# The fourth column group of the down and output products: one 512-column and one 256-column matmul per row block instead of three of 256

## The reference

```python
h = h + g2_l * swiglu_ffn(ada_norm(h, norm_ffn[i], sh2_l, sc2_l), ffn_w_in[i], ffn_w_out[i])   # dn1
h = h + jnp.einsum('bse,ed->bsd', mix, w_out_even[i])                                           # oe
h = h + gated_conv_ffn(hn, w_ffn_gate[layer], ..., w_ffn_down[layer])                           # dn2, dn3
h = h + jnp.einsum('bse,ed->bsd', mix, w_out_odd[i])                                            # oo
```

## Time and profile before

| | us |
|---|---|
| median of three runs | 1526.22 |
| profiled execution, its own time | 1526.18 |
| its span, first to last instruction | 1524.6 |
| PE busy | 1510.4 |
| PE weight loads busy | 1260.0 |
| DVE busy | 938.5 |
| ACT busy | 711.2 |

### The profile page before, as it was taken

One profiled execution on the slowest core, in us unless ns is written; L12 is line 12 of the kernel. 1 busy time (PEld: TensorE's weight loads), 2 busy tenths in 40 slices (PEclk: granted clock), 3 DMA queues, 4 the chain that ended last, 5 costly groups with the idle time before them and its releaser, 6 DMA issues.

```text
span 1524.6 us, 21609 instructions
## 1 busy us (share of the span) xinstructions
PE 1510.4 (99%) x9039; PEld 1260.0 (83%) x9039; DVE 938.5 (62%) x1234; ACT 711.2 (47%) x1002; POOL 76.2 (5%) x103
## 2 busy tenths in 40 slices
PE   7999999999999999999999999999999999999998
PEld 5777657778888888879778888899888899988887
DVE  6332585553424342466877667669789855779973
ACT  5411585342213222245764455545656546556553
POOL 0220041000000000000010000033000000000000
PEclk9999999999999999999999999999999999999999
DMA  9776424452532232453145555665555564565552
GB/s 359 239 206 222 121 32 168 164 194 85 191 111 83 85 108 90 158 194 111 56 166 177 184 188 171 220 201 194 175 197 181 194 193 150 182 203 170 195 191 83
DMA packets 244256, 251.38 MB, mean 165 GB/s; under 512 B 17229, under 2 KB 237744, under 8 KB 244160
## 3 DMA queue, kind: packets, MB, share of 16 engines
q1 hardware_dynamic: 242624, 247.48, 49.3%
q0 software_dynamic: 928, 1.87, 0.4%
q10 hardware_dynamic: 608, 0.66, 0.1%
HBM read 248.94 MB, written 1.05 MB: 164 GB/s over the span
## 4 chain that ended last, share of the span: by engine, by line
PE 98%; DMA 1%; DVE 0%; ACT 0%; issue 0%; SPq 0%; DVEq 0%; ACTq 0%
PE psum L394 95%; PE psum L995 3%; DMA vtok<-in_ctx 1%; PE psum L966 0%; PE psum L563 0%; ACT scr L674 0%; PE psum L2471 0%; DVE sums L1106 0%; ACT L680 0%; PE psum L2351 0%; DVE y L2517 0%; DVE scr L754 0%; DVE xl L745 0%; DVE pt L1128 0%; SPq L298 0%
## 5 line engine op out<-in xcount | busy, mean ns | idle before, releaser
L380 DVE TENSOR_TENSOR wl<-raw,wh 128x2048 fp32r<-128x2048 f32 (+1 forms) x183 | 413.6, 2262 | 251.6 <-ACT wh L373 251.4
L373 ACT ACTIVATE wh<-raw 128x2048 fp32r<-128x2048 f32 (+1 forms) x183 | 344.3, 1883 | 332.8 <-PE psum L394 285.3
L394 PE MATMUL psum<-x,wh 128*128 128x512 f32 (+1 forms) x1520 | 461.6, 364 | 0.0
L394 PE MATMUL psum<-x,wl 128*128 128x256 f32 x1312 | 367.5, 280 | 0.0
L394 PEld LDWEIGHTS psum<-x,wh 128*128 128x128 f32 x1520 | 271.7, 189 | 48.5 <-issue 1.4
L394 PEld LDWEIGHTS psum<-x,wl 128*128 128x128 f32 x1312 | 248.3, 189 | 0.0
L394 PE MATMUL psum<-xh,wh 128*128 128x512 f32 (+1 forms) x624 | 240.5, 385 | 0.3 <-DVE xl L745 0.3
L394 PE MATMUL psum<-xl,wh 128*128 128x512 f32 (+1 forms) x624 | 236.9, 380 | 0.0
L394 PE MATMUL psum<-xh,wl 128*128 128x512 f32 (+1 forms) x624 | 236.8, 380 | 0.0
L394 PEld LDWEIGHTS psum<-xh,wh 128*128 128x128 f32 x624 | 118.1, 189 | 29.4 <-DVE xl L586 4.3
L394 PEld LDWEIGHTS psum<-xh,wl 128*128 128x128 f32 x624 | 118.0, 189 | 22.0
(11 more groups left out here) (290 smaller groups left out, 1990.4 us busy)
## 6 DMA issues: line engine op xcount, KB each, us to landing
raw<-in_ffn_w_in SPq DMA_DIRECT2D x44, 1024.0 KB, 5.0
pre<-in_ada_w SPq DMA_DIRECT2D x27, 1024.0 KB, 9.7
raw<-in_w_ffn_gate SPq DMA_DIRECT2D x22, 1024.0 KB, 5.0
raw<-in_w_ffn_up SPq DMA_DIRECT2D x22, 1024.0 KB, 5.0
raw<-in_ada_w SPq DMA_DIRECT2D x21, 1024.0 KB, 5.4
raw<-in_w_ffn_down SPq DMA_DIRECT2D x19, 1024.0 KB, 4.7
raw<-in_ffn_w_out SPq DMA_DIRECT2D x16, 1024.0 KB, 4.6
raw<-in_na_w_qkv SPq DMA_DIRECT2D x10, 1024.0 KB, 6.6
```

The costliest lines, as they stand in the source:

```text
L373: act.e.activation(wh[:, c % NSPL, 0:z], raw[:, p % NRAW, 0:z], ACT.Copy).then_inc(W.hi, 1)
L380: dve.e.tensor_tensor(wl[:, c % NSPL, 0:z], raw[:, p % NRAW, 0:z], wh[:, c % NSPL, 0:z].bitcast(F32), ALU.subtract).then_inc(W.lo, 1)
L394: return pe.e.matmul(o, l, r, start=start, stop=stop, skip_group_check=shared)
```

## The change

`Down` gets a parameter `wides`, the number of column groups that run wide: four unless said otherwise, three for `o1`, none without a wide operand. `down_pe` and `down_dve` ask for `i < d.wides` where they asked for `i < 3`, and the count of `half` is that of `wides`. So the fourth group of `dn1`, `oe`, `dn2` and `oo` goes through `group_wide` into two banks (6 and 7, 6 and 7, 4 and 5, 6 and 7), and its result is added to the residual in two parts. Everything else stays.

```diff
-            def __init__(self, name, pieces, banks, src, free, gates, gain, to, n, double=False, wide=None):
+            def __init__(self, name, pieces, banks, src, free, gates, gain, to, n, double=False, wide=None, wides=4):
...
-                self.per = 2 if gates else 1
+                self.per, self.wides = 2 if gates else 1, wides if wide is not None else 0
...
-                mine = (3 * self.per if wide is not None else 0, 4 * self.per, ...)
+                mine = (self.wides * self.per, 4 * self.per, ...)
...
         def down_pe(d, ready, ks=None):
             for i in range(4):
                 d.free(i)
-                if d.wide is not None and i < 3:
+                if i < d.wides:
                     group_wide([psum[:, d.banks[i] + m, :] for m in range(2)], d.chunks(i), d.wide, ready, k_outer=i == 0, ks=ks)
...
                 b = bank[d.banks[i]]
-                if d.wide is not None and i < 3:
+                if i < d.wides:
                     parts = [psum[:, d.banks[i]:d.banks[i] + 2, s * T:s * T + T] for s in range(2)]
...
-        O1 = Down("o1", 1, (0, 2, 4, 0), (xh4, xl4), free_o1, (1, 2), None, None, 3, wide=x4)
+        O1 = Down("o1", 1, (0, 2, 4, 0), (xh4, xl4), free_o1, (1, 2), None, None, 3, wide=x4, wides=3)
```

More of the change, by code:

```diff
@@ L1692, in program @@
         class Down:
-            def __init__(self, name, pieces, banks, src, free, gates, gain, to, n, double=False, wide=None):
+            def __init__(self, name, pieces, banks, src, free, gates, gain, to, n, double=False, wide=None, wides=4):
                 self.name, self.pieces, self.banks, self.src, self.free, self.gates, self.wide = name, pieces, banks, src, free, gates, wide
                 self.gain, self.to, self.n, self.double = gain, to, n, double
-                self.per = 2 if gates else 1
+                self.per, self.wides = 2 if gates else 1, wides if wide is not None else 0
                 self.at = downs[-1]
-                mine = (3 * self.per if wide is not None else 0, 4 * self.per, 8 if to else 0, 8 if to and to[1] is not None else 0, 12 if double else 4, 4, 4 if double else 0)
+                mine = (self.wides * self.per, 4 * self.per, 8 if to else 0, 8 if to and to[1] is not None else 0, 12 if double else 4, 4, 4 if double else 0)
                 downs.append(DN._make(a + b for a, b in zip(self.at, mine)))
```

## The result

The changed kernel takes 1529.48 us (median of 13 runs, 1528.41 to 1531.05) against 1526.74 us for the kernel before (13 runs, 1524.23 to 1527.10). The ratio is 1.0025, with a 95% interval of 1.0018 to 1.0032: slower by about 3.8 us (the two medians stand 2.7 us apart), where 1.4 us less was forecast. The profiled execution took 1530.46 us, with a span of 1528.9 us, 4.3 us more than before.

What follows compares the result with a forecast made beforehand. The prediction took PE's stream of matmul pitches as the bound. A gain of 1.47 us less 0.05 us of waiting made -1.42 us, from 1526.22 us to 1524.8 us; the range was 1523.7 to 1526.4 us.

Steps and rivals of the forecast that it cites:

- The gain of the fourth groups: Fourth groups of `dn1`, `oe`, `dn2`, `oo` would take as long as their wide third groups: 1.47 us less.
- The border behind `dn1`: From `dn1` to `even`, PE's spare time before lo of block 6 shrinks to 0.03 us; 0.05 us waiting, bounds 0 and 0.3.
- The other three borders: Behind `oe`, `dn2` and `oo`, the added DVE work of 0.73 us each stays covered, so PE doesn't wait.
- the last of `dn1`'s sums: DVE's sums before PE's statistics behind `dn1`: 2.09 us spare before the change, 1.02 after.
- the span is the sum of PE's matmul pitches, and an edit is worth what it takes out of PE's stream, unless it makes PE wait: Whole kernel: PE's chain is 98% PE, so the edit's worth is PE time removed, 1.47 us, less any new waiting.
- a little slower for a reason that the trace doesn't show: Wide pairs in `oe` took 0.3525 us against 0.3466 in `dn1`; used for the gain's lower end, 0.9 us.
- Columns alone count: PE's column count is unchanged, so no gain: 1526.2 us; chance 0.10 together with the case of covers eaten.
- The chain behind the last add: PE waits for second half-add, hi and lo at all four borders: 3.1 us cost, 1527.8 us; chance 0.04.
- A load paid in full: Each of 120 removed PE weight loads saves its own 189 ns, 22.7 us in all: 1503.5 us; chance 0.01.

Runs made afterwards that it cites:

- SPREAD = 2: The changed kernel with the two transposes that spread the norm factor in `up2` and `up3` two wide pairs later; 1524.62 us, ratio 0.9994.
- STAT = SPREAD = 1: The kernel before with the statistics matmuls and the norm-factor transposes of `up2` and `up3` each one wide pair later; 1531.96 us, ratio 1.0040.

## Why the prediction was wrong

**What held.** The gain of the fourth groups: 1.16 us at once, and 1.46 where `dn2` too keeps the even pace (0.58 in `dn1` of the changed kernel; 0.11, 0.57 and 0.20 in the others with SPREAD = 2, `dn2` 61.02 for 61.59), against 1.47 forecast. The border behind `dn1` became a tie: DVE first, then PE, in the changed kernel.

```profile
1002.89 1.78 DVE L1789 SCALAR_TENSOR_TENSOR hT<-psum,mod,hT 128x256 f32<-128x256 f32 x4
1005.25 0.89 DVE L1723 SCALAR_TENSOR_TENSOR x<-hT,small,x 128x256 fp32r<-128x256 f32 x2 [0.58 <-ACT x L1718]
...
1008.75 0.42 DVE L1744 TENSOR_TENSOR acc<-acc 128x256 f32<-128x256 f32 x1
```

```profile
1005.62 0.28 PE L394 MATMUL psum<-x,wl 128*128 128x256 f32 x1
1005.79 0.50 PE L394 MATMUL psum<-x,wh 128*128 128x256 f32 x2
1006.13 0.28 PE L394 MATMUL psum<-x,wl 128*128 128x256 f32 x1
```

The adds take 1.78 us, lo of block 6 is ready at 1005.25 + 0.48 = 1005.73, and PE, which needed it at 1005.74, starts 0.05 us late (1005.79 for 1005.62 + 0.12), then loses some 0.1 more. `even` is 0.13 us longer; 0.05 had been put there, with 0.3 as the bound. The other three borders show no wait, and the last of `dn1`'s sums, 1008.75 + 0.42 = 1009.17, stayed 1.03 us ahead of PE's statistics at 1010.20. (The prediction's reading of that border before was slightly off: of the eight statistics matmuls the row at 1010.62 in the earlier trace rows shows the last six, and the first starts at 1010.48, so 1.95 us were spare and not 2.09.)

**What failed.** The step by which "the span is the sum of PE's matmul pitches, and an edit is worth what it takes out of PE's stream, unless it makes PE wait". PE did stay the bound, and did not wait. But the step took the pitch of an untouched stage as given, and put what the edit does to `up2`, `dn2` and `up3` at nothing without a reason. The pitch is a state, and the edit passed on another one. The sign of it was in the rows: 0.3525 us per pair in `oe` against 0.3466 in `dn1`, which the prediction put down as "a little slower for a reason that the trace doesn't show", and used only to bound 120 pairs. The same 6 ns on the 880 pairs of `up2`, `dn2` and `up3` is 5.3 us, more than three times the forecast gain, and a look at the starts in `up2`'s first group beside its second would have shown that the pace changes within a stage, at the statistics. The sum with this term put in: -1.47 + (336 + 176 + 336) x 6.6 ns = -1.47 + 5.6, less 0.1 for `up3`'s first group, plus 0.13 for the border: +4.2 us, against 4.19 measured in the seven stages.

**The rivals.** Columns alone count: refuted, the groups got faster by as much as their twins said (that of `dn2` where it has the even pace). The chain behind the last add: right that `dn1`'s border is the thin one, wrong in size, 0.13 us. A load paid in full: refuted. None of them was the mechanism, and the range, up to 1526.4 us, held the first of them and the small terms; the chain's 1527.8 us already lay outside it. The Trainium skill (TensorE: Matmul & The Clock Gate, section Back-to-back issue gap) gives as the isolated gap of one matmul 512 / 2.4 + 2.5 = 215.8 ns and 109.2 ns, an estimate of 325.0 ns per pair, and says itself that in a stream of loads and matmuls both set the spacing. Both steady paces here, 346.7 and 353.3 ns per pair, lie above the estimate, and one number can't give two paces.

**Open.** What in PE makes the pattern of three isn't shown; the runs only show that it exists, what follows a cut, and that moving two to six short instructions by a pair decides it. The statistics behind a 0.236 pair weren't tried.

## What to carry to other kernels

Where PE is the bound, read the pitch of its matmuls in every stage, behind the change too, and not only their number: two stages of the same form with a different mean per pair are a sign that a steady state can be entered or left. Small matmuls that cut into a long even stream set its pace here for more than 100 us; moving them by one or two pairs cost at most 0.1 us per stage by itself, and is worth trying in each of the places of the pattern. A gain of 0.1% that is counted out exactly says little while a state of 0.15 to 0.4% depends on the order of what lies ahead.

## What was not expected of the hardware

- The same sequence of one matmul of 512 and one of 256 columns, each with its load, ran at 0.3467 us per pair (0.230 + 0.117) or at 0.3533 (0.350, 0.361, 0.349 in turn), at the same clock of 1.00. In the changed kernel the slow pattern held from `up2`'s statistics to the end of `dn2`, 1079.3 to 1260.5 us, with nothing changing it, not even the transposes. A third form, 0.350 and 0.344 in turn, has the mean of the fast one; it ran in parts of `up1`, and in `dn1` of three traces, the kernel before among them.
- `dn1`, ahead of every edit but its own, was found at one mean pace or the other from trace to trace: 0.3467 us in five of the eleven profiled kernels, 0.3533 in six. With the wide fourth group it took 61.09 us (the changed kernel, above) or 62.26 us, as in the trace with SPREAD = 2:

```profile
940.38:1002.64 62.26, 62.26 (x354) 54.03 (x354) 38.95 (x38) 32.80 (x33) 0.00 (x0) 1.00 0.64 207
```

- Kernels with the same instructions up to the end of `dn1` differ in its pace (the kernel before has the even mean, the same with STAT = SPREAD = 1 the slow one), so the instructions alone don't decide it. In the last groups of `up1`, ahead of it, PE starts 0.1 to 0.35 us late, by other amounts in each of three traces; that this is what decides `dn1`'s pace isn't shown. Each kernel has one trace only, so how often each pace comes is not known either. The 1.2 us between the two paces of `dn1` are likely a part of the 2 to 3 us between the fastest and the slowest run of one kernel, which leave a difference of 1 us unclear even with ten runs.
